# Loading input pieces in 32 by 32 blocks at their turned place, in a one-core DiT layer kernel

## The reference

```python
x = x + 0.5 * m_lat[:, 2] * swiglu(modulate(rms_norm(x, norm1_g[l]), m_lat[:, 0], m_lat[:, 1]),
                                   ffn1_w_in[l], ffn1_w_out[l])
ctx = ctx + 0.5 * m_ctx[:, 2] * swiglu(modulate(rms_norm(ctx, norm1_g[l]), m_ctx[:, 0], m_ctx[:, 1]),
                                       ffn1_w_in[l], ffn1_w_out[l])
```

## Time and profile before

| | us |
|---|---|
| median of three runs | 2723.37 |
| the profiled execution | 2722.66 |
| its span in the trace | 2720.8 |
| PE busy | 2646.9 (97%) |
| DVE busy | 2138.5 (79%) |
| ACT busy | 1205.8 (44%) |
| POOL busy | 93.8 (3%) |

### The profile page before, as it was taken

How to read it: one execution, slowest core, us unless ns; L and a number is a source line. 1 busy time by engine, 2 the same in 40 slices (tenths; PEclk the granted TensorE clock), 3 DMA queues, 4 the chain that set the end, 5 groups by cost and what they waited for, 6 DMA issues and landing times.

```text
span 2720.8 us, 37858 instructions
## 1 busy us (share of the span) xinstructions
PE 2646.9 (97%) x15259; PEld 2333.5 (86%) x15259; DVE 2138.5 (79%) x2322; ACT 1205.8 (44%) x1362; POOL 93.8 (3%) x131
## 2 busy tenths in 40 slices
PE   5999999999999999999999899999999999999998
PEld 4778999999999998888878888888987888888887
DVE  6869878778787887898887876586677888888766
ACT  6632444444444452231274522465454545454543
POOL 0000111111111100000000000000000000000000
PEclk9999999999999999999999899999999999999999
DMA  9967799999999987676663585442454555555563
GB/s 310 299 200 212 186 250 227 249 244 229 260 233 240 250 237 263 220 252 204 215 233 102 131 266 177 129 121 83 150 171 173 190 196 185 201 207 200 178 217 124
DMA packets 428940, 558.71 MB, mean 205 GB/s; under 512 B 22275, under 2 KB 280697, under 8 KB 428025
## 3 DMA queue, kind: packets, MB, share of 16 engines
q1 hardware_dynamic: 414156, 504.64, 57.5%
q0 software_dynamic: 14384, 51.92, 9.9%
q10 hardware_dynamic: 252, 0.10, 0.0%
HBM read 505.22 MB, written 13.63 MB: 191 GB/s over the span
## 4 chain that ended last, share of the span: by engine, by line
PE 74%; DVE 10%; issue 5%; ACT 4%; DMA 0%; DVEq 0%; ACTq 0%
PE py L1473 13%; PE py L1475 13%; PE py L1474 13%; PE pg L1473 3%; PE pg L1474 3%; PE pg L1475 3%; PE two L1935 2%; DVE sraw L2828 2%; DVE wl L2817 2%; PE two L1936 2%; PE two L1937 2%; DVE wl L2098 1%; PE py L1993 1%; PE py L1994 1%; PE py L1995 1%
## 5 line engine op out<-in xcount | busy, mean ns | idle before, releaser
L2378 DVE TENSOR_TENSOR wl<-raw,wh 128x1024 fp32r<-128x1024 f32 x252 | 307.9, 1222 | 112.2 <-ACT wh L1039 112.1
L1039 ACT ACTIVATE wh<-raw 128x1024 fp32r<-128x1024 f32 x252 | 265.6, 1055 | 288.0 <-DVE raw L2382 228.1
L2098 DVE TENSOR_TENSOR wl<-raw,wh 128x2048 fp32r<-128x2048 f32 x102 | 233.5, 2289 | 140.0 <-ACT wh L894 139.6
L894 ACT ACTIVATE wh<-raw 128x2048 fp32r<-128x2048 f32 x102 | 194.4, 1911 | 204.7 <-PE py L1475 100.5
L1473 PE MATMUL py<-ah,wh 128*128 128x512 f32 x704 | 275.0, 391 | 5.2 <-DVE xy L2484 2.5
L1474 PE MATMUL py<-al,wh 128*128 128x512 f32 x704 | 274.6, 390 | 0.0
L1475 PE MATMUL py<-ah,wl 128*128 128x512 f32 x704 | 274.4, 390 | 0.0
L1473 PE MATMUL py<-hh,wh 128*128 128x256 f32 (+1 forms) x784 | 236.1, 301 | 4.7 <-DVE hl L2176 4.5
L1475 PE MATMUL py<-hh,wl 128*128 128x256 f32 (+1 forms) x784 | 234.4, 299 | 0.0
L1474 PE MATMUL py<-hl,wh 128*128 128x256 f32 (+1 forms) x784 | 234.4, 299 | 0.0
L1090 ACT ACTIVATE wh<-raw 128x2048 fp32r<-128x2048 f32 x44 | 84.3, 1916 | 275.1 <-PE py L1475 275.1
(11 more groups left out here) (503 smaller groups left out, 7105.5 us busy)
## 6 DMA issues: line engine op xcount, KB each, us to landing
raw<-in_ffn_w_out SPq DMA_DIRECT2D x84, 1024.0 KB, 5.1
chunk<-in_ada_w SPq DMA_DIRECT2D x160, 512.0 KB, 5.2
raw<-in_ffn_w_in SPq DMA_DIRECT2D x144, 512.0 KB, 7.5
raw<-in_ffn_w_in SPq DMA_DIRECT2D x58, 1024.0 KB, 5.0
sraw<-in_ffn_w_in SPq DMA_DIRECT2D x40, 1024.0 KB, 5.1
raw<-raw POOLq DMA_DIRECT2D x72, 512.0 KB, 5.8
raw<-in_ada_w SPq DMA_DIRECT2D x64, 512.0 KB
raw<-in_mix_w_in SPq DMA_DIRECT2D x30, 1024.0 KB
```

Of the source, the lines that this page charges most:

```text
L894: nc.scalar.activation(wh[:, slot % 2, :], raw[:, slot, :], ACT.Copy).then_inc(wh_ready, 1)
L1039: nc.scalar.activation(wh[:, slot, o:o + 1024], s_half(k, S_SRC[name]), ACT.Copy).then_inc(wh_ready, 1)
L2098: tt(wl[:, slot % 2, :], raw[:, slot, :], wh[:, slot % 2, :].bitcast(F32), ALU.subtract).then_inc(wl_ready, 1)
L2378: tt(wl[:, slot, o:o + 1024], s_half(k, S_SRC[forms(k)[pos]]), wh[:, slot, o:o + 1024].bitcast(F32), ALU.subtract).then_inc(wl_ready, 1)
```

## The change

Each piece is now loaded in 32 by 32 blocks so that the blocks already lie where the transposed piece has them: of each of `x` and `ctx` four DMAs (b = 0 to 3), each of 32 partitions by 8 by 32 elements, in rows of 32 elements (128 bytes). A piece takes eight DMAs in place of two, and all 16 pieces 128 in place of 32. The transpose within blocks then gives the finished piece in PSUM, and `fold` reads it from there. `spread` on ScalarE and its tile `xq` are gone. The second buffer pair `xp2` lies where `xq` lay, so four pieces have a place in place of two.

On SyncE the pieces stand behind the weight loads of their iteration, and they are issued one pair earlier: pieces 0 to 3 in iteration 29, then two more in each of iterations 30 to 35. Pieces 2 and 3 wait for stores that ended long before, later ones for the turn of the piece that held their place. On VectorE `fold(s)` now comes in iteration s itself, behind `down_low`, and where an iteration has evictions, two of the four banks are evicted ahead of `turn`.

```diff
--- before.py
+++ after.py
@@ -176,7 +176,7 @@
     accm = at("accm", [P, CH], F32, o_xc)
     chunkm = [at(f"chunkm{k}", [P, CH], F32, o) for k, o in enumerate((o_xc + 4 * KB, o_xc + 8 * KB, o_xc + 12 * KB, o_a + 12 * KB))]
 
-    xp = at("xp", [P, 2, 4, P], F32, o_hh)
+    xp = at("xp", [P, 2, TOK], F32, o_hh)
     scratch = nc.dram_tensor("act_scratch", (PAIRS, P, TOK), F32, kind="Internal").ap()
 
     xnat = at("xnat", [P, 4, D], F32, o_xl)
@@ -246,8 +246,8 @@
     act = sm("act", [P, TOK])
     qnl = [at("qnl0", [P, 4, LAT], F32R, o_a + 4 * KB), at("qnl1", [P, 2, LAT], F32R, o_e + 14 * KB),
            at("qnl2", [P, 2, LAT], F32R, small[0])]
+    xp2 = at("xp2", [P, 2, TOK], F32, small[0])
     tv = at("tv", [P, 2, LAT], F32, small[0])
-    xq = at("xq", [P, 2, 4, P], F32, small[0])
     rql = at("rql", [P, 2, LAT], F32R, small[0])
     p1s = at("p1s", [P, 512], F32, small[0])
     rms = sm("rms", [P, TOK])
@@ -295,7 +295,7 @@
     pg, pu = bank("pg"), bank("pu")
     two = nc.alloc_psum_tensor("two", [P, 2, 512], F32)
     pa, pb = two[:, 0], two[:, 1]
-    xt = two[:].rearrange("p a (k c) -> p a k c", k=4)
+    xt = two
     py = [bank(f"py{i}") for i in range(4)]
     pgu = [pg, pu]
     pab = [pa, pb]
@@ -316,8 +316,7 @@
     xsq_ready, xstd_ready, xs_ready = sem("xsq_ready"), sem("xstd_ready"), sem("xs_ready")
     xra_ready, xrv_ready = sem("xra_ready"), sem("xrv_ready")
     wa_loaded, wah_ready, wal_ready, wa_used, fa_done = (sem(n) for n in ("wa_loaded", "wah_ready", "wal_ready", "wa_used", "fa_done"))
-    xp_loaded = [sem("xp_loaded0"), sem("xp_loaded1")]
-    xp_turned, x_spread, x_folded = sem("xp_turned"), sem("x_spread"), sem("x_folded")
+    xp_turned, x_folded = sem("xp_turned"), sem("x_folded")
     rope_loaded = sem("rope_loaded")
     far_loaded = sem("far_loaded")
     raw_loaded = [sem(f"raw_loaded{i}") for i in range(RAW)]
@@ -486,6 +485,9 @@
     LOADED = 16 * (S_PAIRS // 2)
     down_banks = py
 
+    def xp_at(d):
+        return (xp, xp2)[d // 2 % 2][:, d % 2, :]
+
     def raw_turn(m):
         return m // RAW + 1 if m < PROD0 else m // RAW + 1 - TURNS
 
@@ -641,11 +643,15 @@
             def x_piece(d):
                 if d < 2:
                     sp.wait_ge(slab_used, DOWN0 + slot_used_until(11) + 1)
-                else:
-                    sp.wait_ge(xp_turned, d - 1)
-                for src, o in ((x, 0), (ctx, 2)):
-                    sp.dma_start(xp[:, d % 2, o:o + 2, :],
-                                 src[0].rearrange("(k p) c -> p k c", p=P)[:, :, d * P:(d + 1) * P]).then_inc(xp_loaded[d % 2], 16)
+                elif d < 4:
+                    for par in range(2):
+                        sp.wait_ge(act_stored[par], 16 * (PAIRS // 2))
+                else:
+                    sp.wait_ge(xp_turned, d - 3)
+                for src, o in ((x, 0), (ctx, LAT)):
+                    for b in range(4):
+                        sp.dma_start(xp_at(d)[32 * b:32 * b + 32, o:o + LAT].rearrange("j (c i) -> j c i", i=32),
+                                     src[0].rearrange("(c j) i -> j c i", j=32)[:, :, d * P + 32 * b:d * P + 32 * b + 32]).then_inc(x_loaded[d % 4], 16)
 
             def b_next(n):
                 kind, k = B_LOADS[n - 4]
@@ -657,12 +663,15 @@
 
             n = 4
             for j in range(len(STEPS)):
-                if X_STEP - 1 <= j < X_STEP + 7:
-                    x_piece(2 * (j - X_STEP) + 2)
-                    x_piece(2 * (j - X_STEP) + 3)
                 while n < len(B_LOADS) and B_LOADS.index(("w", min(j + 2, len(STEPS) - 1))) >= n - 4:
                     b_next(n)
                     n += 1
+                if j == X_STEP - 1:
+                    x_piece(0)
+                    x_piece(1)
+                if X_STEP - 1 <= j < X_STEP + 6:
+                    x_piece(2 * (j - X_STEP) + 4)
+                    x_piece(2 * (j - X_STEP) + 5)
                 chunks_ahead(B_CHUNKS[j])
             assert n == len(B_LOADS)
 
@@ -938,19 +947,6 @@
                 o = part * LAT
                 se.wait_ge(nt_ready, TILES[stage] - KT + part * KT + t + 1)
                 nc.scalar.activation(hh[:, part, t, :], nt[:, t % 2, o:o + LAT], ACT.Identity, bias=shift[:, t:t + 1]).then_inc(hh_ready, 1)
-
-            def spread(s):
-                se.wait_ge(xp_turned, 2 * s + 2)
-                if s:
-                    se.wait_ge(x_folded, 2 * s)
-                else:
-                    for par in range(2):
-                        se.wait_ge(act_stored[par], 16 * (PAIRS // 2))
-                for row in range(4):
-                    for col in range(4):
-                        ins = nc.scalar.activation(xq[32 * col:32 * col + 32, :, :, 32 * row:32 * row + 32],
-                                                   xt[32 * row:32 * row + 32, :, :, 32 * col:32 * col + 32], ACT.Copy)
-                ins.then_inc(x_spread, 1)
 
             def token_stats(k):
                 se.wait_ge(x_loaded[k], 16)
@@ -1124,8 +1120,6 @@
                     static_split(MIX0 + j + 2 - len(STEPS))
                 if 8 <= r < 11:
                     squares(r)
-                if 0 <= s < 8:
-                    spread(s)
             roots(0)
             def project(s, out_ap, in_ap):
                 se.wait_ge(slab_used, MIX0 + s + 1)
@@ -2299,20 +2293,18 @@
 
             def turn(s):
                 for d in (2 * s, 2 * s + 1):
-                    ve.wait_ge(xp_loaded[d % 2], 32 * (s + 1))
+                    ve.wait_ge(x_loaded[d % 4], 16 + 128 * (d // 4 + 1))
                 if s:
-                    ve.wait_ge(x_spread, s)
+                    ve.wait_ge(x_folded, 2 * s)
                 for d in (2 * s, 2 * s + 1):
-                    nc.vector.transpose(xt[:, d % 2].rearrange("p k c -> p (k c)"),
-                                        xp[:, d % 2].rearrange("p k c -> p (k c)")).then_inc(xp_turned, 1)
+                    nc.vector.transpose(xt[:, d % 2, :], xp_at(d)).then_inc(xp_turned, 1)
 
             def fold(s):
-                ve.wait_ge(x_spread, s + 1)
                 for d in (2 * s, 2 * s + 1):
+                    ve.wait_ge(xp_turned, d + 1)
                     ve.wait_ge(y_free, Y_F1 + KT + d + 1)
-                    x_ = xq[:, d % 2].rearrange("p k c -> p (k c)")
                     for part, gate in ((0, g1l), (1, g1c)):
-                        ins = stt(xy[:, part, d, :], xy[:, part, d, :], gate[:, d:d + 1], x_[:, part * LAT:(part + 1) * LAT], ALU.mult, ALU.add)
+                        ins = stt(xy[:, part, d, :], xy[:, part, d, :], gate[:, d:d + 1], xt[:, d % 2, part * LAT:(part + 1) * LAT], ALU.mult, ALU.add)
                     ins.then_inc(x_folded, 1)
 
             def whole(dst, part, t0):
@@ -2471,9 +2463,9 @@
             pair_gate(PAIRS - 1)
             down_low(1)
 
-            def add_out(j):
+            def add_out(j, ds=range(4)):
                 part, q, _ = STEPS[j]
-                for d in range(4):
+                for d in ds:
                     k = 4 * q + d
                     if d < 3:
                         ve.wait_ge(y_done, 12 * part + 3 * q + d + 1)
@@ -2504,12 +2496,13 @@
                     amp(a2l, 4, ml, V_N2)
                     amp(a2c, 4, mc, V_N2)
                     amp(a3l, 7, ml, V_N3)
-                if 1 <= s <= 8:
-                    fold(s - 1)
+                evict = step_last(j) and STEPS[j][0]
+                if evict:
+                    add_out(j, (0, 1))
                 if 0 <= s < 8:
                     turn(s)
-                if step_last(j) and STEPS[j][0]:
-                    add_out(j)
+                if evict:
+                    add_out(j, (2, 3))
                 if r == 11:
                     square_adds(r)
                 if j + 2 < len(STEPS):
@@ -2518,6 +2511,8 @@
                     down_low(j + 2)
                 else:
                     static_split(MIX0 + j + 2 - len(STEPS))
+                if 0 <= s < 8:
+                    fold(s)
                 if 8 <= r < 11:
                     square_adds(r)
                 if j > 1 and LATE_M - 1 in B_CHUNKS[j - 2]:
```

## The result

The kernel after the change took 2727.93 us (median of 15 runs, 2725.92 to 2730.49), the kernel before, run beside it, 2722.81 us (15 runs, 2720.53 to 2723.53). The ratio is 1.0020, with a 95% interval of 1.0012 to 1.0027: 5.1 us slower, just inside the 0.2% that the prediction called no change, and 1.2 us above its number. The profiled execution took 2726.87 us with a span of 2725.1 us, 4.2 and 4.3 us more than before; the mean granted clock is 0.992.

What follows compares the result with a forecast made beforehand. TensorE, busy 97%, bounds the kernel, so only its waits count. +6.2 us ahead of step 32 and -2.9 at steps 35 and 38 give +3.3, so 2726.7 us; own range 2724 to 2729, 8 in 10 within 2718.5 to 2736.

Steps and rivals of the forecast that it cites:

- What bounds: TensorE, busy 97% of the span: only its three waits for VectorE's evictions matter in this stage, 7.3 us together.
- The first turn: On VectorE, the first turn waits 6.2 us for pieces 0 and 1, whose 16 issues start 0.51 us apart.
- The chunk: Iteration 30's second chunk load, issued behind 32 blocks, makes VectorE wait another 1.1 us before the first eviction.
- The clock "is lost as before": Ahead of step 32, TensorE's longer pause loses no more clock than the old one, with the same return from the lower level.
- The two waits at steps 35 and 38: TensorE's waits there vanish because `fold` no longer waits for `spread`: -2.9 us.
- SyncE's lag of about 10 us is made good without a further wait: In later iterations 16 blocks take 8.2 us, 9.3 with other loads, of a 10.88 us step.
- Packets hidden: On the DMA queue, 128-byte packets cost 10 to 19 ns; the first 32 blocks' 7.7 us hides within 16.3 of issuing.
- The sum: Over the stage, +6.2 us ahead of step 32 and -2.9 at steps 35 and 38 give +3.3 us.
- Rival A: On SyncE, blocks issue in about 0.25 us, so pieces arrive for the old turn: -6.0 us, 2717.4 us; chance 0.16.
- Rival B: SyncE's 32 issues ahead of iteration 29's chunk loads bound: slower from 0.58 us each, 2732.8 us at 0.70; chance 0.26.
- Rival C: On the DMA queue, 128-byte packets cost 38 ns by read-modify-write: about +24 us, 2747 us at the dearest; chance 0.07.
- D: The first eviction comes as late as before, so only 2.9 us are gained: 2720.5 us; chance 0.09.

Runs made afterwards that it cites:

- e1: Kernel after, but each piece loaded by two DMAs of the old shape again (permuted residual), all else of the change kept; 2722.69 us, ratio 1.0002.
- e9: e1 with the pieces ahead of the weight load on SyncE again (residual still permuted); 2717.41 us, ratio 0.9982.
- e2b: Kernel after with the same 128 DMAs, each in 32 rows of 1 KB instead of 256 of 128 bytes (wrong residual); 2724.23 us, ratio 1.0008.
- e8: e5 with pieces 2 and 3 issued in ScalarE's iteration 27 instead of 29, whole computation kept; 2717.13 us, ratio 0.9983.
- e6: Kernel before with only two evictions moved ahead of the turn, loads and `spread` untouched; 2718.28 us, ratio 0.9987.
- e5: Kernel after with all 128 block DMAs issued by ScalarE, pieces 0 and 1 in iteration 28, 2 and 3 in 29; 2718.42 us, ratio 0.9989.
- e7: e5 with the turn ahead of all four evictions again; 2721.58 us, ratio 1.0.
- e3: Kernel after with the blocks of pieces 0 and 1 issued in SyncE's iteration 28 instead of 29; 2722.63 us, ratio 1.0003.
- e10: Kernel after with all blocks behind SyncE's chunk loads, pieces 2 and 3 in iteration 27, 0 and 1 in 28; 2723.08 us, ratio 1.0003.
- e4: Kernel after with iteration 29's chunk loads between the blocks of pieces 0, 1 and of pieces 2, 3; 2727.87 us, ratio 1.0019.

## Why the prediction was right, and where its terms were off

- **What bounds.** Right. TensorE's pauses in this stage, each behind an eviction, are what the change moved; the difference of the steps' lengths gives the 4.7 us.
- **The first turn** was to wait 6.2 us: 6.38. The step rests on 16 issues and a landing. The blocks are issued 0.49 us apart, not 0.51, and two issues were long and not one, so the last of the 16 was issued 9.2 us after the first and not 8.6; it landed in 2.0 us and not 2.5. The two errors cancel, so the closeness of the number is in part luck. That the weight load ahead of them costs 2.8 us even with the old DMAs (e1) stood in the prediction only as a later start, not as a term.
- **The chunk** was to add 1.1 us: 1.15. TensorE's pause was to be 8.7 us: 8.7. That VectorE's waits carry over one to one is borne out by e9 against e1: 2.83 us of waiting there moved the pause from 1.3 to 4.1.
- **The clock "is lost as before"** was mis-sized. The windows of the kernel after, with the clock in the column after the engines' busy times:

```profile
1366.00:1370.00 4.00, 0.00 (x0) 0.00 (x0) 2.85 (x3) 0.00 (x0) 0.00 (x0) 0.50 1.01 375
...
1371.00:1375.00 4.00, 4.00 (x10) 3.14 (x11) 4.00 (x6) 1.91 (x1) 0.00 (x0) 0.50 1.00 288
1375.00:1376.00 1.00, 1.00 (x4) 0.81 (x3) 1.00 (x2) 0.00 (x0) 0.00 (x0) 0.51 0.47 73
1376.00:1379.00 3.00, 3.00 (x14) 2.45 (x14) 3.00 (x4) 0.00 (x0) 0.00 (x0) 1.00 0.42 66
```

  TensorE works from 1370.85 to 1376 at 1.2 GHz, 5.1 us, which at half speed is 2.6 us lost. Before, 0.57 over 4 us is 3.4 us at that level, 1.7 us lost. Step 32 is 22.25 = 10.88 + 8.7 + 2.7, and was 15.29 = 10.88 + 2.5 + 1.9: 0.8 us more than the forecast had. The clock had also fallen at another moment: now during the pause (0.50 from 1366 on), before only after TensorE had resumed.
- **The two waits at steps 35 and 38** were to go, -2.9 us: -1.46 and -0.80. The step that failed is "SyncE's lag of about 10 us is made good without a further wait", which took 8.2 us for 16 blocks. They took 12.6 us (1365.43 to 1378.02), the first eight of them while the weight load ahead was still moving, so SyncE fell behind: five later turns waited, and 0.4 us of pause remained at step 38. With long rows (e2b) no later turn waited.
- **Packets hidden**, and a small packet no dearer than a larger one: right as far as it went. From 1353 to 1361, where only blocks move, the queue shows

```profile
q1 hardware_dynamic: 4460, 0.54, 43.5%
```

  which is 0.435 x 8 us x 16 / 4460 = 12.5 ns a packet, within the 10 to 19 estimated. What the prediction missed is that issues with many small rows behind a large load are held up.
- **The sum** was +3.3 us; the steps give +4.7. The 1.4 between them are 0.8 of clock and 0.6 at step 38. The runs say +5.1. The number 2726.7 came within 1.2 us in part because it was counted from a median of three runs that lay 0.6 above that of the runs made beside the kernel after.
- **Rival A** (the cover holds, -6.0) did not come, but its mechanism is real: with the loads in time e8 and e9 gain 4.5 and 4.2 us. Of its 1.3 us pause "no lost clock shows" was right: step 32 is then 12.5 us (e6, e9), 0.3 beyond pause and step, as with the pauses of 1.2 us before, and the granted clock stays at 1.00. **Rival B** named the right place and 0.58 us per issue as the point of decision; the average there was (1363.37 - 1345.63) / 32 = 0.55 us, a little short of it. **Rival C** is out by the 12.5 ns. **D** is out: the eviction came later.

Open: what the removal of `spread` is worth by itself (e9 and e6 leave it at about half a microsecond, within their intervals); whether blocks on SyncE ahead of the weight load would do as well as e8; and how late `act_high` is in the executions of e5 and e7 that were not profiled.

## What to carry to other kernels

A DMA cut into four costs four issues, so price the queue of the issuing engine in order, with all that stands ahead and behind, before the bytes. An engine without slack passes every wait on in full, so look there first for what a load's later issue delays. A change with two parts of opposite sign looks like no change: run each part alone, since here two moved lines were worth 3.7 us and the rest had buried them.

## What the runs showed of the hardware

- An issue on SyncE takes about the same for 256 rows of 128 bytes (0.49 us apart) as for 32 rows of 1 KB (0.46), but behind a weight load of 1 MB it lengthens with many rows, up to 2.5 us for one:

```profile
L653 SPq DMA_DIRECT2D xp<-in_x x64: 311/452/2507, 1345.6 to 1437.6; - x64
```

  With long rows the longest was 1.4 us, at a DMA share as high. ScalarE's issues lengthen too: 12.4 us for 16 in e5, where 16 others took 8.1 (1329.89 to 1337.99).
- A pause of TensorE costs more than itself, and in steps rather than in proportion. Taken from the length of step 32 less 10.88 and the pause: 1.3 us of pause cost 0.3 more (e6, e9); 2.5, 3.6 and 4.1 us cost 1.8 to 1.9 (before, e3, e1); 4.5, 6.0, 8.6 and 8.7 us cost 2.7 to 3.1 (e10, e2b, e4, after). The granted clock says why: after 1.3 us it stayed at 1.00, after 2.5 to 4.1 us TensorE worked for about 3.4 us at 1.2 GHz, and after the longer pauses for 5 to 6 us. So a pause cut from 2.5 to 1.3 us gave back 2.8 us. (In e5, e7 and e8 ScalarE's copies do not start at the ends of the steps, so they are not in this list.)
